# A two-layer decoder trunk: token-tile flow between the layers, and all conditioning pieces summed by VectorE

## The chip, the cores and the metric

The kernel runs on one core of a Trainium2 chip. The metric is the device time of one execution in microseconds (us). Three runs of the kernel before took 1729.4, 1731.59 and 1733.0 us.

## The reference, cut to what matters

The reference computes two layers (DEPTH = 2) over 512 tokens of width 1024, all in f32. A conditioning vector c of 1024 numbers is multiplied in each layer with a matrix `ada_w` of 1024 x 6144. The product, in twelve pieces of 512 columns, gives shift, scale and gate of both sub-layers:

```
mods = silu(c) @ ada_w[l] + ada_b[l]          # sh1, sc1, g1, sh2, sc2, g2: two pieces each
h  = rms_norm(x, norm_mix_w) * (1 + sc1) + sh1
x  = x + g1 * mixer(h)                        # attention + mLSTM, gated merge, one output projection
h2 = rms_norm(x, norm_ffn_w) * (1 + sc2) + sh2
x  = x + g2 * grouped_moe(h2)                 # 16 experts, two for each token
```

Each expert has three matrices of 1024 x 512 or 512 x 1024 (2 MB each), and the tokens are sorted by expert into blocks of 64 rows.

## The kernel before, in words

Five engines each run a program of their own and meet by semaphores. One loop over the layers (`Fori(0, DEPTH)`) holds a whole layer on each engine. Tokens are cut into NT = 4 tiles of 128, features into KD = 8 chunks of 128.

The head of a layer norms x tile by tile (`head_norm`: ScalarE squares, VectorE scales the sum, GpSimd takes the power -0.5, ScalarE writes the normed rows to `xn`). TensorE multiplies pieces 0 to 3 of `ada_w` with c (`head`, L868 to L886), turns them into columns, and VectorE forms the scale `A1` (`head_mod`, L1291). For layer 1 this head runs at the end of layer 0. Then the layer ends with a meeting: each engine waits for all five, clears its share of the semaphores, and waits again (`layer_end`, L351). At the start of the layer TensorE transposes `xn`, one feature chunk of all four tiles at a time into one of two PSUM banks (L912 to L917), and ScalarE and VectorE write `hT`.

The mixer's products all go through two PSUM banks, `pj[0]` and `pj[1]`, in an order written out in `group_order` (L39). Group g uses bank g % 2, and `take` (L890) makes TensorE wait until every earlier group of that bank has been freed:

```
if g >= 2:
    pe.wait_ge(pj_free[g % 2], g // 2)
return pj[g % 2]
```

The first merge loop (L1064 on TensorE, L1547 on VectorE, j = 0 to 7) makes the gate product `ga`, two steps of the mLSTM and the attention's up projection `ya`. VectorE reads `ya` out at L1557. With j = 2, 4 and 6 it first finishes a token tile of the mLSTM (`m_finish`, L1519). Then come `gb` 0 and 1 and four transposed tiles `hmT` (L1074 to L1079; read out at L1562). The second merge loop (L1080, L1564) makes `gb` and `yb`; `gb` 0 and 1 stand ahead of the loop, so `yb` 0 and `yb` 1 follow each other directly. VectorE reads `yb` out at L1568, and GpSimd adds it to the merged features (L538).

In the second merge loop VectorE also sums six conditioning pieces (4 to 9): `sum_mid` (L1538) is one `tensor_scalar` and seven `scalar_tensor_tensor` over 128 x 512. TensorE then sums over the partitions with a product with ones (L1093, or four column sums, L865), and VectorE stores the outcome (`mod_chunk`, L1320). Pieces 10 and 11 are multiplied by TensorE (`ada_group`, L902), one before the transposes of h2 and one beside the routing.

SyncE issues the loads of the weights from a list `ITEMS` (L272) into a ring of six buffers of 2 MB. It issues the experts' gate and up matrices, the parameters of the next layer (`params`, L368, before the loads of the last expert), and the four pieces for the next layer's head. GpSimd issues the experts' down matrices: for experts 0 and 2 after the second merge loop, for expert 1 when the first rows of the experts' stage have been transposed (L567 to L569). After the last block GpSimd gathers both expert rows of each tile (L576), and VectorE adds them to x (`combine`, L1713).

## Time and profile before

| | us |
|---|---|
| median of three runs | 1731.59 |
| the three runs | 1729.4, 1731.59, 1733.0 |
| span of the profiled execution | 1724.8 |
| TensorE busy | 1506.9 |
| VectorE busy | 563.9 |
| ScalarE busy | 323.4 |
| GpSimd busy | 121.8 |

The page gives no time of its own for the profiled execution beside its span; the span runs from the first to the last instruction, and the median of the runs is 6.8 us above it. In time a layer has these stages (layer 0): head to 53.4 us, projections and attention to 243, first merge loop to 347, second merge loop to 442, output projection to 497, routing and the scatter of the rows to 546, experts to 841, and the passage to the next layer to 893. Layer 1 repeats it 839.6 us later as far as the routing.

### The profile page before, as it was taken

What the parts mean: (1) busy time and instruction counts of PE and PEld (TensorE: products, weight loads), DVE (VectorE), ACT (ScalarE), POOL (GpSimd) and SP (SyncE); (2) the same over time, 40 slices, a digit from 0 to 9 for tenths busy, and PEclk for the clock granted to TensorE, in tenths of its full rate; (3) what the DMA queues carried; (4) which work ended last, traced back from release to release, by engine and by line L of the source; (5) the groups of instructions that cost most, each with busy time, mean ns of one, the idle gap of its engine ahead of it and who ended that gap; (6) DMA issues with size and microseconds to landing.
All of it is one profiled execution on the core that took longest, in us unless ns stands there. A gap on an engine that the chain in (4) does not pass through costs nothing.

```text
span 1724.8 us, 18335 instructions
## 1 busy us (share of the span) xinstructions
PE 1506.9 (87%) x5819; PEld 669.3 (39%) x5820; DVE 563.9 (33%) x1459; ACT 323.4 (19%) x809; POOL 121.8 (7%) x157
## 2 busy tenths in 40 slices
PE   4999999999983999987749999999999387999982
PEld 1544444544441333332335444454444132333330
DVE  1346432446333212111134554243642411221213
ACT  3133411200011212111132343111000121221210
POOL 1100000011101000000111000000110100000001
PEclk8999999999996999999769999999999789999996
DMA  9822111055747899999952111113563799997984
GB/s 307 338 97 98 49 49 49 13 206 173 291 142 268 268 375 379 376 388 360 322 180 98 49 49 50 49 49 108 206 224 145 292 314 381 378 354 247 310 303 165
DMA packets 160813, 366.59 MB, mean 213 GB/s; under 512 B 12433, under 2 KB 14705, under 8 KB 160753
## 3 DMA queue, kind: packets, MB, share of 16 engines
q1 hardware_dynamic: 127568, 256.26, 42.2%
q0 software_dynamic: 21664, 83.89, 12.8%
q10 hardware_dynamic: 11520, 25.70, 5.0%
q8 instruction: 31, 0.51, 0.1%
q14 instruction: 30, 0.24, 0.0%
HBM read 334.37 MB, written 31.46 MB: 212 GB/s over the span
## 4 chain that ended last, share of the span: by engine, by line
PE 69%; DMA 11%; SPq 5%; DVE 5%; issue 4%; ACT 2%; POOL 2%; ACTq 0%; DVEq 0%; POOLq 0%; PEldq 0%
PE bank L939 23%; PE bank L1160 14%; PE bank L929 11%; PE bank L1105 6%; PE bank L1172 6%; DMA weight_ring<-in_w_up_dram 6%; DMA regA<-in_w_up_dram 2%; SPq L428 2%; SPq L431 2%; SPq L371 2%; DMA weight_ring<-in_ada_w_dram 1%; PE bank L1152 1%; PE bank L999 1%; POOL expert_rows L558 1%; PE bank L988 1%
## 5 line engine op out<-in xcount | busy, mean ns | idle before, releaser
L939 PE MATMUL bank<-h_features,weight_ring 128*128 128x512 f32 x768 | 342.4, 599 | 3.1 <-ACT regB L674 1.9
L1160 PE MATMUL bank<-weight_ring,merged_features 128*64 128x512 f32 x960 | 227.2, 628 | 35.3 <-DMA weight_ring<-in_w_up_dram 28.2
L939 PEld LDWEIGHTS bank<-h_features,weight_ring 128*128 128x128 f32 x768 | 144.8, 192 | 182.7 <-issue 182.4
L929 PE MATMUL bank<-weight_ring,h_features 128*128 128x512 f32 (+1 forms) x512 | 196.1, 541 | 1.7 <-ACT h_features L628 1.7
L1703 DVE TENSOR_TENSOR merged_features<-bank,merged_features 64x512 f32<-64x512 f32 x44 | 30.5, 693 | 381.8 <-ACT merged_features L809 381.8
L1160 PEld LDWEIGHTS bank<-weight_ring,merged_features 128*64 128x64 f32 x960 | 73.5, 144 | 165.4 <-issue 160.8
L929 PEld LDWEIGHTS bank<-weight_ring,h_features 128*128 128x128 f32 x512 | 96.0, 190 | 97.0 <-issue 91.6
L1160 PE MATMUL bank<-h_features,merged_features 128*64 128x512 f32 x256 | 117.1, 612 | 11.0 <-DMA regA<-in_w_up_dram 10.0
L1160 PE MATMUL bank<-regA,merged_features 128*64 128x512 f32 x256 | 117.5, 614 | 0.0
L1105 PE MATMUL bank<-weight_ring,merged_features 128*128 128x512 f32 x256 | 110.4, 593 | 3.0 <-POOL merged_features L538 3.0
L1172 PE MATMUL bank<-weight_ring,merged_features 128*64 128x512 f32 x480 | 109.6, 598 | 1.6 <-DVE merged_features L1689 1.6
L809 ACT ACTIVATE merged_features<-bank 64x512 f32<-64x512 f32 x46 | 27.1, 589 | 367.9 <-PE bank L1160 367.9
L1152 PE MATMUL bank<-ident,merged_features 64*128 64x64 f32 x384 | 34.9, 233 | 44.5 <-DMA merged_features<-expert_rows 44.5
L800 ACT ACTIVATE merged_features<-bank,mod_cols,scale 128x64 f32<-128x64 f32 x192 | 61.9, 402 | 60.6 <-PE bank L1152 58.3
L1105 PEld LDWEIGHTS bank<-weight_ring,merged_features 128*128 128x128 f32 x256 | 48.5, 190 | 63.4 <-issue 60.2
L1544 DVE SCALAR_TENSOR_TENSOR regP<-weight_ring,c_padded,regP 128x512 f32<-128x512 f32 x84 | 63.2, 752 | 3.0
L1160 PEld LDWEIGHTS bank<-h_features,merged_features 128*64 128x64 f32 x256 | 34.8, 141 | 73.7 <-issue 73.7
L1685 DVE TENSOR_SCALAR merged_features<-bank,scale,mod_cols 128x64 f32<-128x64 f32 x192 | 52.8, 338 | 27.1 <-PE bank L1152 25.5
L1689 DVE TENSOR_TENSOR merged_features<-bank,g_rows 128x512 f32<-128x512 f32 x46 | 31.8, 692 | 89.8 <-PE bank L1172 78.9
L1152 PEld LDWEIGHTS bank<-ident,merged_features 64*128 64x128 f32 x384 | 28.2, 142 | 82.0 <-DMA merged_features<-expert_rows 44.7
L939 PE MATMUL bank<-regB,weight_ring 128*128 128x512 f32 x128 | 57.4, 594 | 1.6 <-DVE regB L1562 1.6
L939 PE MATMUL bank<-regA,weight_ring 128*128 128x512 f32 x128 | 57.6, 592 | 0.0
(304 smaller groups left out, 1376.1 us busy)
## 6 DMA issues: line engine op xcount, KB each, us to landing
weight_ring<-in_ada_w_dram SPq DMA_DIRECT2D x24, 2048.0 KB, 8.7
weight_ring<-in_w_gate_dram SPq DMA_DIRECT2D x22, 2048.0 KB, 21.1
weight_ring<-in_w_down_dram POOLq DMA_DIRECT2D x22, 2048.0 KB, 14.9
weight_ring<-in_w_up_dram SPq DMA_DIRECT2D x22, 2048.0 KB, 20.4
weight_ring<-in_w_in_dram SPq DMA_DIRECT2D x18, 2048.0 KB, 8.9
h_features<-in_w_gate_dram SPq DMA_DIRECT2D x10, 2048.0 KB, 17.4
regA<-in_w_up_dram SPq DMA_DIRECT2D x10, 2048.0 KB, 27.4
regB<-in_w_down_dram POOLq DMA_DIRECT2D x10, 1536.0 KB, 11.5
```

The source lines that it names most:

```text
L371: sp.dma_start(dst, src).then_inc(params_in, 16)
L428: sp.dma_start(gate_w[p], of(w_gate, l, e)).then_inc(w_gu[p], 16)
L431: sp.dma_start(up_w[p], of(w_up, l, e)).then_inc(w_gu[p], 16)
L800: last = ac.activation(xT[:, k, :], ps[2][:, MB * k:MB * k + MB], ACT.Identity, scale=A2[:, k:k + 1], bias=modc[:, 24 + k:25 + k])
L929: ins = te.matmul(bank[:, 0:w], hT[:, k, P * i:P * i + P], wv[:, k, :], start=(k == 0), stop=(k == KD - 1))
L939: ins = te.matmul(bank[:, :], wv[:, k, c0:c0 + P], rhs[:, k, :], start=(k == 0), stop=(k == kn - 1))
L1105: ins = te.matmul(bank[:, :], merged[:, k, P * i:P * i + P], slot("wo", k // 4, 4, D)[:, k % 4, 512 * h:512 * h + 512], start=(k == 0), st ...
L1152: ins = te.transpose(ps[(2, 6)[k % 2]][:, MB * k:MB * k + MB], xg[p][:, P * k:P * k + P], ident[MB * p:MB * p + MB, MB * p:MB * p + MB])
L1160: ins = te.matmul(ps[3][64 * part:64 * part + 64, :], xT[:, k, :], w[:, k, :], start=(k == 0), stop=(k == KD - 1))
L1172: ins = te.matmul(ps[5][64 * half:64 * half + 64, :], hxT[:, k, :], down_w[p][k][:, 512 * half:512 * half + 512], start=(k == 0), stop=(k ...
L1544: link(ve.scalar_tensor_tensor(mid_sum, w[:, k, :], cz[:, k, 0:1], mid_sum, ALU.mult, ALU.add))
L1685: last = ve.tensor_scalar(xT[:, k, :], ps[6][:, MB * k:MB * k + MB], A2[:, k:k + 1], modc[:, 24 + k:25 + k], ALU.mult, ALU.add)
```

## The change

Conditioning. All twelve pieces are now summed by VectorE in the merge loops: pieces 4 to 11 of this layer and pieces 0 to 3 of the next one (`STREAM`; in layer 1 the last four are computed too, and not used). Four pieces are summed in the first merge loop, half a piece behind each `ya`, the others in the second, one ahead of `hmT` and one behind each of `yb` 0 to `yb` 6. The pieces are loaded into the place of x and into `regA`; x is written to memory at the start of the layer and read back after the last piece. TensorE's sums over the partitions stand in `group_order` behind `ya` 2, 4 and 6, `gb` 0 and each `yb`. `mod_chunk`, which frees their bank, now stands behind the sum of a later piece. TensorE multiplies only the four pieces of layer 0's head.

Between layers. The meeting is gone: the semaphores are in two sets, and SyncE clears each when the engines have reported themselves through. At the start of a layer TensorE transposes one token tile after another into banks 4 to 7, tiles 0 and 1 first, tiles 2 and 3 between `q` 0 and `kv` 0. The weights `q` and `kv` of layer 1 are loaded at the end of layer 0.

Experts. Down matrices of experts 0 and 1 are loaded after the second merge loop and of expert 2 after the output projection. The parameters of the next layer are loaded at the start of the experts' stage. The two experts of a token are now ordered by their slot; the rows of the lower one are gathered when expert 14's blocks are stored. The gate weights are worked out behind the slots and tables.

```diff
+STREAM = [(0, c) for c in range(HEAD_ADA, 12)] + [(1, c) for c in range(HEAD_ADA)]
+N_HALVED = 4
+ADA_AT = {("ya", 2): 0, ("ya", 4): 1, ("ya", 6): 2, ("gb", 0): 3, ("yb", 0): 4, ("yb", 1): 5, ("yb", 2): 6, ("yb", 3): 7,
+          ("yb", 4): 8, ("yb", 5): 9, ("yb", 6): 10, ("yb", 7): 11}
+ADA_SLOT = ("x", "x", "x", "x", "A", "x", "A", "x", "A", "x", "A", "x")
...
     for j in range(8):
-        o += [("ga", j), ("ya", j)]
-    o += [("gb", 0), ("gb", 1)]
+        o += [("ga", j), ("ya", j)] + sums("ya", j)
+    o += [("gb", 0)] + sums("gb", 0) + [("gb", 1)]
...
-        o += [("yb", j)]
-        if j - 1 in MID_ADA:
-            o += [("ada", MID_ADA[j - 1])]
+        o += [("yb", j)] + sums("yb", j)
...
# SyncE
+                wait_reg(sp, head_xn, l * NT + NT)
+                sp.dma_start(xsave.rearrange("(i p) d -> p i d", p=P), xs[:, :, :]).then_inc(x_kept, 16)
...
+                through(sp, "ya", 7)
+                load_ada(4)
+                summed(sp, 3)
+                load_ada(5)
                 load_gate(0, 0)
-                through(sp, "yb", 0)
...
+                through(sp, "hmT", NT - 1)
+                load(l, "wo0")
+                for n in range(6, len(STREAM)):
+                    summed(sp, n - 2)
+                    load_ada(n)
+                    if n == 7:
+                        load(l, "wo1")
+                    if n == 9:
+                        through(sp, "gb", 3)
+                        load_gate(1, 1)
+                summed(sp, len(STREAM) - 1)
+                sp.dma_start(xs[:, :, :], xsave.rearrange("(i p) d -> p i d", p=P)).then_inc(x_back, 16)
...
# GpSimd
-                through(pool, "ada", G2_ADA + 1)
-                pool.wait_ge(xt_ready, 1)
-                load_down(1, 1)
...
-                wait_reg(pool, y_out, nb * 32 + 32)
-                for i in range(NT):
-                    for k in range(2):
+                for k in range(2):
+                    wait_reg(pool, y_out, (nb if k else blocks_through(po, E - 2)) * 32 + 32)
+                    for i in range(NT):
...
# TensorE, head of layer 0
+            param_columns(0)
+            pe.wait_ge(head_read, 1)
+            head_mods()
...
# TensorE, both loops
+                def mod_sum(n):
+                    summed(pe, n)
+                    bank = take("ada", n)
+                    if STREAM[n][1] in (4, 5, 10, 11):
+                        ins = te.matmul(bank[:, :], ones[:, :], sum_buf(n), start=True, stop=True)
+                    else:
+                        ins = column_sums(bank, sum_buf(n))
+                    ins.then_inc(pj_ready, 1)
...
+                h1_transposes(0)
+                h1_transposes(1)
                 for i in range(NT):
+                    pe.wait_ge(h1_low, i + 1)
+                    pe.wait_ge(h1_high, i + 1)
                     token_group("q", i, 512)
+                    if i == 0:
+                        h1_transposes(2)
+                        h1_transposes(3)
                     token_group("kv", i, 256)
...
# VectorE, first merge loop, behind the read-out of ya
+                    sum_ada(j // 2, slice(0, 4) if j % 2 == 0 else slice(4, KD))
+                    if ("ya", j) in ADA_AT:
+                        mod_chunk(ADA_AT["ya", j])
                 m_state(15)
                 m_finish(NT - 1)
+                mod_chunk(ADA_AT["gb", 0])
+                sum_ada(N_HALVED)
                 for i in range(NT):
...
# VectorE, second merge loop, behind the read-out of yb
-                    if j - 1 in MID_ADA:
-                        mod_chunk(MID_ADA[j - 1])
-                    if j in MID_ADA:
-                        sum_mid(MID_ADA[j])
-
+                    if N_HALVED + 1 + j < len(STREAM):
+                        sum_ada(N_HALVED + 1 + j)
+                    mod_chunk(ADA_AT["yb", j])
+
+                wait_reg(dve, x_back, l * 16 + 16)
...
# VectorE, end of the layer
-                    head_mod(l + 1)
+                    head_cols(l + 1)
+                    head_mod(modn[:, :])
                     for i in range(NT):
-                        combine(i)
+                        combine(0, i)
+                    for i in range(NT):
+                        combine(1, i)
+                        ve.sem_inc(combined, 1)
                         if i:
                             head_norm(l + 1, i - 1)
                     head_norm(l + 1, NT - 1)
```

## Rows read from the trace of the kernel before

**Rows 1.** Page, part 1: busy us, share of the span, instructions
```profile
PE 1506.9 (87%) x5819; PEld 669.3 (39%) x5820; DVE 563.9 (33%) x1459; ACT 323.4 (19%) x809; POOL 121.8 (7%) x157
```

**Rows 2.** Timeline of PE and DVE, first merge loop, layer 0: start us, us, line
```profile
283.50 7.03 PE L939 MATMUL bank<-h_features,weight_ring 128*128 128x512 f32 x16
287.11 0.69 DVE L1557 SCALAR_TENSOR_TENSOR merged_features<-merged_features,bank 128x512 f32<-128x512 f32 x1 [0.23 <-DVE regP L1516]
...
334.69 7.03 PE L939 MATMUL bank<-h_features,weight_ring 128*128 128x512 f32 x16
338.26 0.69 DVE L1557 SCALAR_TENSOR_TENSOR merged_features<-merged_features,bank 128x512 f32<-128x512 f32 x1 [0.23 <-DVE regB L1509]
```

**Rows 3.** Timeline of PE and DVE, second merge loop, layer 0
```profile
347.52 0.69 DVE L1557 SCALAR_TENSOR_TENSOR merged_features<-merged_features,bank 128x512 f32<-128x512 f32 x1 [2.67 <-PE bank L939]
...
354.10 0.69 DVE L1535 TENSOR_TENSOR weight_ring<-weight_ring,fin_small 128x512 f32<-128x512 f32 x1
...
365.35 7.13 PE L939 MATMUL bank<-regB,weight_ring 128*128 128x512 f32 x16 [0.78 <-DVE regB L1562]
...
373.48 1.52 DVE L1542 TENSOR_SCALAR regP<-weight_ring,c_padded 128x512 f32<-128x512 f32 x1 [0.26 <-DVE regU L1568]
375.04 5.48 DVE L1544 SCALAR_TENSOR_TENSOR regP<-weight_ring,c_padded,regP 128x512 f32<-128x512 f32 x7
...
382.62 1.02 PE L1093 MATMUL bank<-regP,ones 128*128 128x512 f32 x2
...
390.66 3.60 PE L939 MATMUL bank<-regB,weight_ring 128*128 128x512 f32 x8
```

**Rows 4.** Timeline of all engines, passage from layer 0 to layer 1
```profile
848.36 1.00 POOL L578 DMA_INDIRECT h_features<-expert_rows,slot_index  x1 [48.29 <-DMA expert_rows<-merged_features]
...
860.76 1.29 DVE L1716 SCALAR_TENSOR_TENSOR x_tokens<-h_features,gate_weights,x_tokens 128x1024 f32<-128x1024 f32 x1 [0.24 <-DVE scale L1299]
...
874.00 0.15 DVE L1288 TENSOR_SCALAR sum_sq<-sum_sq 128x1 f32<-128x1 f32 x1 [1.13 <-ACT merged_features L600]
...
885.04 0.06 DVE L1342 MEMSET regU<- 128x6 f32 x1 [10.89 <-issue]
...
892.98 19.40 PE L929 MATMUL bank<-weight_ring,h_features 128*128 128x512 f32 x57 [0.87 <-ACT h_features L628]
```

**Rows 5.** Timeline of POOL and PE, start of the experts, layer 1
```profile
1385.47 0.80 POOL L541 DMA_DIRECT2D weight_ring<-in_w_down_dram  x1 [9.60 <-PE bank L1152]
...
1424.60 7.09 PE L1160 MATMUL bank<-weight_ring,merged_features 128*64 128x512 f32 x32
...
1441.18 8.78 PE L1160 MATMUL bank<-weight_ring,merged_features 128*64 128x512 f32 x32 [4.88 <-DMA weight_ring<-in_w_up_dram]
```

**Rows 6.** Chain of waits, 860 to 895: start us, us, what
```profile
877.31 3.32 issue
```

**Rows 7.** Windows, experts of layers 0 and 1: busy, then PEclk, DMA share, GB/s
```profile
799.00:810.00 11.00, 9.87 (x52) 4.01 (x54) 2.17 (x6) 2.24 (x6) 0.75 (x1) 1.00 1.08 333
...
1441.00:1459.00 18.00, 13.43 (x62) 5.18 (x63) 2.49 (x6) 2.26 (x6) 0.74 (x1) 0.89 1.04 385
```

**Rows 8.** Timeline of PE, last expert of layer 0
```profile
822.89 9.10 PE L1160 MATMUL bank<-weight_ring,merged_features 128*64 128x512 f32 x32 [11.07 <-DMA weight_ring<-in_w_up_dram]
```

**Rows 9.** Timeline of DVE, routing, layer 0
```profile
521.11 0.23 DVE L1645 TENSOR_TENSOR regP<-regP 128x64 f32<-128x64 f32 x1
...
522.75 0.24 DVE L1654 COPY regP<-bank 128x80 f32<-128x80 f32 x1
```

**Rows 10.** Timeline, end of layer 1
```profile
1694.48 0.69 DVE L1689 TENSOR_TENSOR merged_features<-bank,g_rows 128x512 f32<-128x512 f32 x1 [4.40 <-DMA expert_rows<-merged_features]
1699.22 1.00 POOL L578 DMA_INDIRECT h_features<-expert_rows,slot_index  x1 [39.04 <-DMA expert_rows<-merged_features]
...
1705.89 1.28 DVE L1716 SCALAR_TENSOR_TENSOR x_tokens<-h_features,gate_weights,x_tokens 128x1024 f32<-128x1024 f32 x1 [10.71 <-DMA regA<-expert_rows,slot_index]
```

**Rows 11.** Timeline of DVE, head of layer 0
```profile
28.88 0.29 DVE L1294 COPY param_cols<-bank 128x128 f32<-128x128 f32 x1
```

More of the change, by code:

```diff
@@ L295, in mix_item @@
-            if name == "wo":
-                return lay(w_out, l)[:, 512 * part:512 * part + 512, :].rearrange("a (k p) n -> p (a k) n", p=P), D, 4
-            return cols8({"ya": w_attn_up, "yb": w_mlstm_up}[name], l, 0, D), D, 4
-        def slot(name, part, k, w):
-            return ring[:, ITEMS[ITEM[(name, part)]][2], 0:k * w].rearrange("p (k n) -> p k n", k=k)
-        def before(n):
-            return [it[2] for it in ITEMS[:n]].count(ITEMS[n][2])
+                return slot(name, 8, w), cols8(w_in, l, c0, w)
@@ new lines, in _ @@
+                sp.dma_start(xsave.rearrange("(i p) d -> p i d", p=P), xs[:, :, :]).then_inc(x_kept, 16)
+                sp.wait_ge(head_sum, HEAD_ADA)
+                for name in ("mqk0", "mqk1", "mv", "mo"):
+                    load(l, name)
+                wait_reg(sp, x_kept, l * 16 + 16)
+                load_ada(0)
+                with sp.If(l == 0):
+                    sp.wait_ge(zeroed, 3)
+                    sp.dma_start(xd.rearrange("(n p) d -> p n d", p=P),
+                                 zeros.unsqueeze(1).to_broadcast([P, ROWS // P, D])).then_inc(rows_zeroed, 16)
@@ new lines, in _ @@
+                through(sp, "q", NT - 1)
+                load(l, "ga0")
+                wait_reg(sp, moe_done, l * 4 + 4)
+                for done in moe_sems:
+                    sp.sem_clear(done)
+                sp.sem_inc(moe_cleared, 1)
+                through(sp, "mqk", 7)
+                load(l, "ga1")
+                through(sp, "mv", NT - 1)
+                load(l, "ya")
+                through(sp, "mo", NT - 1)
+                load(l, "yb")
+                summed(sp, 0)
+                load_ada(1)
@@ L427, in load_gate @@
+                through(sp, "ga", 3)
+                load(l, "gb0")
+                summed(sp, 1)
+                load_ada(2)
+                summed(sp, 2)
+                load_ada(3)
+                through(sp, "ga", 7)
+                load(l, "gb1")
                 def load_gate(p, e):
@@ L449, in _ @@
                 load_up(2, 2)
+                with sp.If(l < DEPTH - 1):
+                    sp.wait_ge(x_upd, NT)
+                    params(nxt)
+                wait_reg(sp, mix_done, l * 4 + 4)
+                for done in mix_sems:
+                    sp.sem_clear(done)
+                sp.sem_inc(mix_cleared, 1)
                 with sp.Fori(1, E // BUF) as i:
@@ L1278, in hlink @@
                 dve.wait_ge(head_step, hn[0])
-            def columns(j, bank, read, lnk):
-                lnk(ve.tensor_copy(modc[:, 4 * j:4 * j + 4], bank[:, 0:4]))
-                ve.sem_inc(read, 1)
             def head_norm(t, i):
@@ L1344, in _ @@
                 link(ve.tensor_scalar(wqk[:, 0, :], wqk[:, 0, :], HD ** -0.5, None, ALU.mult))
[L1345 to L1347 removed]
+                for i in range(NT):
+                    dve.wait_ge(h1_ready, 2 * i + 2)
+                    for k in range(4, KD):
+                        ins = ve.tensor_scalar(hT[:, k, P * i:P * i + P], h1_bank(i, 1)[:, P * (k - 4):P * (k - 4) + P], A1[:, k:k + 1], modc[:, k:k + 1],
+                                               ALU.mult, ALU.add)
+                    ins.then_inc(h1_high, 1)
                 nh = HQ + HKV
@@ L1730, in _ @@
                     for i in range(NT):
-                        combine(i)
-                layer_end(dve, l, share(4))
+                        combine(0, i)
+                    for i in range(NT):
+                        combine(1, i)
+                        ve.sem_inc(combined, 1)
+                dve.sem_inc(moe_done, 1)
 def program(nc, args):
```

457 lines of the change are left out of this document (224 added, 233 removed).

## The prediction, made before the changed kernel was timed

> **What bounds the kernel now.** I read the page first: TensorE is busy 87% of the span, VectorE 33% [rows 1]. So in the mixer the question is whether each added or moved instruction makes TensorE wait, and only in the passages between stages does another engine set the pace. I then read the timeline stage by stage. The reader is to see four things. In the first merge loop VectorE reads `ya` out late where it has just finished an mLSTM tile: `ya` ends at 283.5 and is read out by 287.8, and TensorE does not mind, since the next product goes to the other bank [rows 2]. In the second loop TensorE runs without gaps, one step from 382.62 to the next `yb` at 390.66 [rows 3]. Between the layers TensorE makes no large product from about 841 to 893; what passes is gathers, additions to x, norms, the meeting and the transposes [rows 4, 6]. In the experts' stage TensorE waits for weights where experts with one block follow each other [rows 5, 8].
>
> **The first merge loop: slower.** The change puts a sum over partitions behind `ya` 2, 4 and 6. It takes one group number, so the next `ga` is three groups behind its predecessor and falls on the bank of `ya` itself, where it was on the other bank. `take` then waits for VectorE's read-out of `ya`. These are exactly the three steps with `m_finish` ahead of the read-out. For j = 2 the read-out ends at 287.11 + 0.69 = 287.8; with 0.15 to pass the semaphore `ga` starts at 287.95 where it started at 283.5, 4.45 late. For j = 6 it is 338.26 + 0.69 + 0.15 - 334.69 = 4.4 [rows 2]. The partition sum itself (1.0, as L1093 in rows 3) lies inside this wait. Three steps by 4.5 us are 13.5 a layer, 27 in all. The half sums (four operations, 3.1 by rows 3) run behind the read-out beside `ga` (7.0) and cost nothing; the bank of the partition sum is free before the next `ya`. If the wait were hidden after all, 1.0 would be left of each, 6 in all; if each is a little longer (the middle one), 30.
>
> **hmT and the second merge loop: slower.** Follow VectorE from the last `ya`, read out at 348.2 [rows 3]. Half sum 3.1: 351.3. The last mLSTM steps took 354.8 - 348.2 = 6.6: 357.9. Then the new whole sum of a piece stands ahead of `hmT`. A sum is 0.7 to 1.5 for L1542 and 5.48 for seven L1544 [rows 3], here 6.2 since GpSimd is idle: 364.2. The transposed tiles are read out in some 3 us, two of them already in banks: `yb` 0 starts at 367.4, not 365.35, 2.1 late. (Piece 4 is issued at 347.4 and has 10.5 us to land; it may be late by some us.) `yb` 0 ends at 370.85, is read out by 371.75, and now the next sum runs at once, beside GpSimd's addition of `yb` 0. That is the case of the row at 373.48, where L1542 took 1.52; 0.26 + 1.52 + 5.5 gives 379.05. Only then come `mod_chunk` and the read-out of `yb` 1, whose bank `gb` 2 needs: 380.1 against 372.3 before, 7.8 late. A further sum (7.0) and `mod_chunk` must pass before `yb` 2: 387.6 against 379.2, 8.4 late. In the five steps that follow VectorE's own period decides: from the end of a `yb`, 0.2 + 0.7 + 0.26 + 7.0 + `mod_chunk` + 0.1 is 8.5 us with columns and 9.0 with rows, until the bank of the next `yb` is free, against 8.04 now [rows 3]. Three steps by 0.45 and two by 0.98 are 3.3. Together 11.7 a layer, 23.4 in all. Bounds: 4 if only the two added partition sums a layer count, 35 if pieces also arrive 6 us late in each layer. The way of x through memory is hidden: it is read back 6 us before `wo` begins, and the first `wo` group gives another 7.
>
> **Between the layers: faster.** The head's four pieces of `ada_w` no longer load beside the last stores, nor does VectorE wait for their columns. In layer 1, where nothing loads beside them, a first store and the read-out behind it let the gathers start 4.7 after the last row block [rows 10]; I take the same here, gathers of the lower slot from 842.0 and of the upper one from 847.1, against 848.36 for all [rows 4]. From the first gather of a pair to the first addition it was 6.7 there (1699.22 to 1705.89), that is 5.4 from the second, as issues are 1.3 apart; so tile 0 gets its second addition at 852.6, where before its first began at 860.76. From 860.76 to VectorE's last norm at 874.00 it was 13.2, with eight additions of 1.3. Four of these are now ahead (5.2), of which ScalarE's squares and scalings give back about half: 10.4, so 863.0. Now a choice. VectorE's first instruction of layer 1 stands at 885.04, and the chain has "issue" from 877.31 on, when ScalarE too was done; that is 7.7 us in which nothing is waited for [rows 4, 6]. I keep these 7.7, as the loop still jumps back: VectorE resumes at 870.7, has two small operations and four read-outs of tile 0, and `q` 0 starts at 872.6. Eight transposes each of tiles 2 and 3 now stand inside the projections (2.3), and the first products after an idle stretch cost 2.0 more (9.10 against 7.09 in rows 5 and 8). 892.98 - 872.6 - 4.3 is 16.1 gained. If the 7.7 belonged to the meeting it would be some 22; if gathers and stores keep their old times, 10.
>
> The Trainium skill ("Runtime: NRT & Kernel Launch", section "Instruction fetch mechanics") says that a taken branch out of the fetched pages forces a fetch before execution goes on. By that rule the 7.7 us stay whatever is done with the meeting, and `q` 0 can't start when the first tile is ready; without it the passage would gain some 6 us more. The row at 885.04 fits the rule but can't by itself tell it from the meeting.
>
> **Other places.** Experts of layer 1: expert 1's down matrix was issued at 1385.47, into the stretch in which the transfers are the limit; 2.1 MB at 385 GB/s are 5.5 us [rows 5, 7], and the wait of 4.88 and the one of the next expert can give them back: 5.5 (between 0 and 6). Layer 0 begins with experts of two blocks, whose products cover the loads, so there this gives nothing; but the parameters leave the stretch ahead of the last expert, whose weights come 11.07 late [rows 8]. Their bytes (0.67 MB, 1.7 us) and the dip from 385 to 333 GB/s over 11 us (1.5) make 3.2 (0 to 11). Routing: seven operations leave the path between the mask and the ranks, 521.11 to 522.75 [rows 9], and four products go: 1.3 a layer, 2.6. TensorE's pieces 10 and 11 lay in its own waits: nothing. End of layer 1: the gathers run from 1695, when the block before the last is stored, instead of 1699.22, and one addition of 1.3 instead of two follows the last of them [rows 10]: 4.2 + 1.3 = 5.5 (3 to 8). Head of layer 0: the pieces are now multiplied behind the read-out of the parameters at 28.88 [rows 11] instead of from 18.8, some 4 late, and transposing by tile gives about as much back: 0, between -3 and +3.
>
> **The sum.** Slower by 27 + 23.4 = 50.4; faster by 16.1 + 5.5 + 3.2 + 2.6 + 5.5 = 32.9. The span goes from 1724.8 to 1742.3. The median of the runs stands 6.8 above the span, so 1749.
>
> **The rivals.** (A) The banks do not bite, and the passage wins. Place: TensorE's waits for banks in both loops. If late read-outs cost only the partition sums, 27 becomes 6 and the 3.3 a layer of the second loop go: 27.6 less, 1721.5. It decides once the loops lose less than 33 in all. For it speaks that VectorE is busy only 33% [rows 1], so that much of its work could be ahead; against it the numbering of the banks, which is arithmetic. (B) The waits cool TensorE. Each new wait idles it for 3.4 to 3.9 us. In layer 1 a product group after 4.88 us without work took 8.78 instead of 7.09, at a mean granted clock of 0.89 in that stretch, so part of it at the lower level of 1.2 GHz [rows 5, 7]. Five such waits a layer by 1.7 are 17: 1766. Against it: these idle times are shorter than that one. (C) The pieces arrive late. Two buffers alternate, a load is issued when a sum ends and has 15.9 us; expert weights and `wo` share the queue. If each of six loads a layer came 4 us late it would be 48 more: 1797. Against it: before, the sums in rows 3, from two buffers too, wait for no load.
>
> **Chances.** What a measurement can tell here is about 0.2%, 3.5 us. My forecast 0.60 (its own range 1735 to 1762, 0.05 of it within 3.5 us of before), (A) 0.20 (0.03 of it within), (B) 0.15, (C) 0.05. So slower 0.75, within 0.2% 0.08, faster 0.17. The range for 8 in 10 goes from 1725 to 1766.
>
> **What would show it.** Right: TensorE idle before L939's successor three times a layer in the first loop, released by VectorE's read-out of `ya`; seven VectorE sums of 7 us back to back in the second loop; `wo` starting some 25 us later relative to `q`; VectorE silent for about 7.7 us at the start of layer 1; no wait of TensorE for the meeting. Wrong: first-loop steps still 12.9 us apart at j = 2, 4, 6; VectorE resuming within 1 us of its last norm; waits for `ada_w` loads in the loops.

## The result and the profile after

The changed kernel takes 1772.49 us (median of 4 runs, 1767.85 to 1779.8) against 1730.49 (median of 4, 1729.32 to 1733.0): ratio 1.0237, 95% interval 1.0207 to 1.0267. It is 42 us slower; the forecast was 1749, in a range of 1725 to 1766. The direction was right, the size was not.

The profiled execution took 1779.8 us, with a span of 1778.2, so it stands 7 above the median of its kernel. For the stages below that means: the spans differ by 53.4 us, the medians by 42; the 11 between are differences from run to run, not effects of the change.

Page of the kernel after, busy times and the clock that TensorE was granted, in 40 slices of the span:

```profile
PE 1513.3 (85%) x5723; PEld 673.7 (38%) x5724; DVE 642.0 (36%) x1581; ACT 324.8 (18%) x825; POOL 123.9 (7%) x157
...
PEclk9999989899996899999779998999999869899996
```

The same row of the kernel before:

```profile
PEclk8999999999996999999769999999999789999996
```

TensorE has fewer products but more busy time than before [rows 1]. The clock's row shows where to look. The first merge loop of layer 0 runs from slice 6 to slice 9, and slices 6 and 8 read 8 where they read 9 before. Slice 8 holds two of the new waits. Slice 6 ends before the first of them; what is slow there is `ga` 0 (see below). Tenths over 44 us are too coarse for the rest; windows below show it.

Where the time went, each stage from start to start, in both traces:

| stage | before | after | change | forecast |
|---|---|---|---|---|
| layer 0, start to `q` 0 | 53.4 | 45.6 | -7.8 | 0, with the next row |
| layer 0, `q` 0 to `ga` 0 | 190.1 | 193.7 | +3.6 | |
| layer 0, first merge loop (to `gb` 0) | 104.3 | 126.0 | +21.7 | +13.5 |
| layer 0, `gb` 0 to `wo` | 94.6 | 112.8 | +18.2 | +11.7 |
| layer 1, both loops | 199.0 | 236.1 | +37.1 | +25.2 |
| both layers, `wo`, routing, scatter | 208.0 | 206.1 | -1.9 | -2.6 |
| layer 0, experts | 294.8 | 295.2 | +0.4 | -3.2 |
| last product to `q` 0 of layer 1 | 51.9 | 31.0 | -20.9 | -16.1, with the next row |
| layer 1, `q` 0 to `ga` 0 | 190.0 | 195.2 | +5.2 | |
| layer 1, experts, to the last product group | 304.3 | 308.2 | +3.9 | -5.5 |
| layer 1, end | 34.4 | 28.2 | -6.2 | -5.5 |

(The stages of experts end with the last product in layer 0 and with the start of the last group in layer 1; what follows is counted from there.) The loops cost 77.0 and not 50.4; the rest gives back 23.7 and not 32.9.

Timeline of the first merge loop, layer 0, kernel after (start us, us, engine, line; in brackets the idle time before it and what ended it), answering to [rows 2]:

```profile
280.74 1.02 PE L965 MATMUL bank<-regU,ones 128*128 128x512 f32 x2
...
284.35 0.69 DVE L1619 SCALAR_TENSOR_TENSOR merged_features<-merged_features,bank 128x512 f32<-128x512 f32 x1 [0.23 <-DVE regP L1587]
...
285.19 8.80 PE L998 MATMUL bank<-h_features,weight_ring 128*128 128x512 f32 x16 [3.42 <-DVE merged_features L1619]
...
312.68 1.02 PE L965 MATMUL bank<-regU,ones 128*128 128x512 f32 x2
317.51 10.13 PE L998 MATMUL bank<-h_features,weight_ring 128*128 128x512 f32 x16 [3.81 <-DVE merged_features L1619]
...
350.50 8.80 PE L998 MATMUL bank<-h_features,weight_ring 128*128 128x512 f32 x16 [3.45 <-DVE merged_features L1619]
```

The waits stand where the forecast put them: behind the partition sum of `ya` 2, 4 and 6, ended by the read-out of `ya`, and with the sum itself 13.7 us in layer 0 and 13.6 in layer 1, against 13.5 foreseen. What it did not count is the second number of these rows: the product group behind the wait takes 8.80 and 10.13 us instead of 7.03. Windows over two of these groups and one between them (busy times, then the granted clock, DMA share, GB/s):

```profile
285.20:294.00 8.80, 8.80 (x18) 3.82 (x19) 3.19 (x5) 0.00 (x0) 0.00 (x0) 0.81 0.01 2
299.80:306.80 7.00, 7.00 (x19) 3.10 (x18) 3.61 (x5) 0.00 (x0) 0.00 (x0) 1.00 0.42 130
317.50:327.60 10.10, 10.09 (x18) 4.29 (x19) 3.20 (x5) 0.00 (x0) 0.00 (x0) 0.70 0.01 2
```

Mean clock 0.81 and 0.70 with the transfers quiet: part of each group ran at 1.2 GHz and the rest at 2.4, right behind 3.4 to 3.8 us without a product. Three groups cost 1.77 + 3.10 + 1.77 = 6.6 us in layer 0. In layer 1 the first of the three takes 8.80 too, and the other two:

```profile
1180.92 8.51 PE L998 MATMUL bank<-h_features,weight_ring 128*128 128x512 f32 x16 [3.78 <-DVE merged_features L1619]
...
1212.27 9.89 PE L998 MATMUL bank<-h_features,weight_ring 128*128 128x512 f32 x16 [3.42 <-DVE merged_features L1619]
```

That is 6.1 us, and here the longer wait has the faster group: the cost of one wait scatters between 1.5 and 3.1 us and does not follow its length.

`ga` 0 is slow without any wait. It stands ahead of the first added sum, behind products with four rows; first the kernel before, then the kernel after:

```profile
243.48 8.73 PE L939 MATMUL bank<-h_features,weight_ring 128*128 128x512 f32 x16
```

```profile
232.51 5.40 PE L1095 MATMUL bank<-merged_features,ident 4*128 4x512 f32 x8 [0.25 <-ACT weight_ring L776]
...
239.34 9.97 PE L998 MATMUL bank<-h_features,weight_ring 128*128 128x512 f32 x16
```

From 231.0 to 239.3 TensorE of the changed kernel is busy for 8.05 of 8.30 us at a mean clock of 0.73. In the twelve kernels of this study `ga` 0 takes between 8.6 and 10.2 us, in either layer, and the products of four rows ahead of it 3.9 to 5.6. In this pair of profiles the place costs 2.1 us in the stage `q` 0 to `ga` 0 and 1.2 in the first loop more than before. The instructions there are the same in both kernels, and e6 (below) is back at 3.94 and 8.79. I count these 3.3 us as scatter and not as an effect of the change; what sets them no run shows.

Second merge loop, kernel after, answering to [rows 3]:

```profile
384.64 5.40 PE L998 MATMUL bank<-regB,weight_ring 128*128 128x512 f32 x8 [0.78 <-DVE regB L1629]
...
391.03 1.52 DVE L1404 TENSOR_SCALAR regP<-x_tokens,c_padded 128x512 f32<-128x512 f32 x1 [0.26 <-DVE regU L1635]
...
398.58 1.74 PE L921 MATMUL bank<-ones,regP 128*128 128x1 f32 x8 [3.94 <-DVEq L1393]
400.18 9.76 PE L998 MATMUL bank<-h_features,weight_ring 128*128 128x512 f32 x16
...
422.71 3.67 PE L998 MATMUL bank<-regB,weight_ring 128*128 128x512 f32 x8 [1.23 <-DVEq L1393]
```

Again the foreseen waits (the partition sum behind `yb` 1, and each later `yb` behind `mod_chunk`, L1393) and slow products: `yb` 0 5.40 instead of 3.60, behind three short waits of the transposes and of itself (0.34, 0.95 and 0.78 us), the partition sum behind `yb` 1 1.74 instead of 0.95, `gb` 2 9.76 instead of 7.03. That is 5.3 us; 18.2 less 5.3 is 12.9 against 11.7 foreseen. In layer 1 `yb` 0 takes 3.70 behind nearly the same three waits (0.34, 0.92 and 0.78), the sum 1.84 and `gb` 2 9.23, so that only 3.1 us are lost to the clock there.

The passage, kernel after, answering to [rows 4]:

```profile
878.42 1.00 POOL L635 DMA_INDIRECT h_features<-expert_rows,slot_index  x1 [38.85 <-DMA expert_rows<-merged_features]
...
884.06 1.28 DVE L1788 SCALAR_TENSOR_TENSOR x_tokens<-h_features,gate_weights,x_tokens 128x1024 f32<-128x1024 f32 x1 [5.19 <-DMA h_features<-expert_rows,slot_index]
...
900.89 0.15 DVE L1338 TENSOR_SCALAR sum_sq<-sum_sq 128x1 f32<-128x1 f32 x1 [2.25 <-ACT merged_features L657]
...
905.50 0.06 DVE L1410 MEMSET regU<- 128x6 f32 x1 [4.46 <-issue]
...
907.51 1.22 PE L987 MATMUL bank<-weight_ring,h_features 128*128 128x512 f32 x1 [5.73 <-ACT h_features L680]
```

The gathers begin 1.9 us behind the last product (876.5), the last norm stands at 900.9, and VectorE resumes 4.46 us later, waiting for nothing that the profile shows.

Experts of layer 1, kernel after, answering to [rows 5, 7]:

```profile
1441.75 9.46 PE L1216 MATMUL bank<-weight_ring,merged_features 128*64 128x512 f32 x32 [1.38 <-ACT merged_features L857]
...
1518.56 1.08 PE L1216 MATMUL bank<-h_features,merged_features 128*64 128x512 f32 x1 [14.58 <-DMA regA<-in_w_up_dram]
```

Expert 5's up matrix is waited for 14.58 us, where before expert 4 waited 4.88 [rows 5] and expert 5 4.39:

```profile
1458.96 1.08 PE L1160 MATMUL bank<-h_features,merged_features 128*64 128x512 f32 x1 [4.39 <-DMA regA<-in_w_up_dram]
```

The end of layer 1, kernel after, answering to [rows 10]:

```profile
1753.68 1.00 POOL L635 DMA_INDIRECT h_features<-expert_rows,slot_index  x1 [33.85 <-DMA expert_rows<-merged_features]
...
1767.32 1.28 DVE L1788 SCALAR_TENSOR_TENSOR x_tokens<-regA,gate_weights,x_tokens 128x1024 f32<-128x1024 f32 x1 [1.98 <-DMA regA<-expert_rows,slot_index]
```

The lower slot's gathers and additions run ahead of the last stores, as foreseen (6.2 against 5.5).

### The profile page after: what moved, and what is told of

It is laid out like the page before. It is cut to its first block, busy times and chain, and to the rows that moved or that the text cites. A ratio compares the mean times of both kernels' runs of the same rounds, so it can differ in the third digit from the quotient of the medians.

```text
span 1778.2 us, 18326 instructions
## 1 busy us (share of the span) xinstructions
PE 1513.3 (85%) x5723; PEld 673.7 (38%) x5724; DVE 642.0 (36%) x1581; ACT 324.8 (18%) x825; POOL 123.9 (7%) x157
## 4 chain that ended last, share of the span: by engine, by line
PE 63%; DMA 13%; DVE 11%; issue 6%; ACT 3%; POOL 2%; SPq 1%; DVEq 0%; POOLq 0%; ACTq 0%
PE bank L998 18%; PE bank L1216 15%; PE bank L987 11%; DMA weight_ring<-in_w_up_dram 8%; PE bank L1228 6%; PE bank L1164 5%; DVE regP L1406 3%; DMA regA<-in_w_up_dram 2%; PE bank L1208 1%; DVE regP L1404 1%; DMA expert_rows<-merged_features 1%; PE bank L1065 1%; SPq L469 1%; DMA regA<-expert_rows,slot_index 1%; PE bank L1054 1%
## 5 line engine op out<-in xcount | busy, mean ns | idle before, releaser
L998 PE MATMUL bank<-h_features,weight_ring 128*128 128x512 f32 x768 | 363.1, 628 | 24.5 <-DVE merged_features L1619 21.3
L1216 PE MATMUL bank<-weight_ring,merged_features 128*64 128x512 f32 x960 | 229.7, 634 | 27.4 <-DMA weight_ring<-in_w_up_dram 20.3
L998 PEld LDWEIGHTS bank<-h_features,weight_ring 128*128 128x128 f32 x768 | 151.2, 201 | 215.3 <-issue 214.9
L1216 PE MATMUL bank<-h_features,merged_features 128*64 128x512 f32 x256 | 116.1, 607 | 21.9 <-DMA regA<-in_w_up_dram 20.9
L1216 PEld LDWEIGHTS bank<-weight_ring,merged_features 128*64 128x64 f32 x960 | 73.5, 145 | 160.0 <-issue 155.3
L1228 PE MATMUL bank<-weight_ring,merged_features 128*64 128x512 f32 x528 | 120.6, 598 | 1.6 <-DVE merged_features L1762 1.6
L1208 PEld LDWEIGHTS bank<-ident,merged_features 64*128 64x128 f32 x384 | 28.2, 142 | 80.2 <-DMA merged_features<-expert_rows 42.9
L1228 PEld LDWEIGHTS bank<-weight_ring,merged_features 128*64 128x64 f32 x528 | 35.4, 136 | 60.1 <-issue 58.0
## 6 DMA issues: line engine op xcount, KB each, us to landing
weight_ring<-in_w_gate_dram SPq DMA_DIRECT2D x22, 2048.0 KB, 14.8
```

Source lines behind the costliest of these rows:

```text
L998: ins = te.matmul(bank[:, :], wv[:, k, c0:c0 + P], rhs[:, k, :], start=(k == 0), stop=(k == kn - 1))
L1208: ins = te.transpose(ps[(2, 6)[k % 2]][:, MB * k:MB * k + MB], xg[p][:, P * k:P * k + P], ident[MB * p:MB * p + MB, MB * p:MB * p + MB])
L1216: ins = te.matmul(ps[3][64 * part:64 * part + 64, :], xT[:, k, :], w[:, k, :], start=(k == 0), stop=(k == KD - 1))
L1228: ins = te.matmul(ps[5][64 * half:64 * half + 64, :], hxT[:, k, :], down_w[p][k][:, 512 * half:512 * half + 512], start=(k == 0), stop=(k ...
```

## The experiments

The theory: the loss is the bank of `ya`, held by a late read-out, and each such wait also costs clock. The rivals: it is the summing itself that makes VectorE late; the slow products have another cause than the wait. Ratios are to the kernel before, run on the same chip; the changed kernel's is 1.0237.

**The partition sums moved (e1).** VectorE sums as much, at the same places; only the groups of TensorE and their read-outs move.

```diff
-ADA_AT = {("ya", 2): 0, ("ya", 4): 1, ("ya", 6): 2,
+ADA_AT = {("ya", 3): 0, ("ya", 5): 1, ("ya", 7): 2,
```

> The changed kernel with the three partition sums of the first merge loop behind ya 3, 5 and 7 instead of ya 2, 4 and 6; nothing else. ga still falls on the bank of the ya before it, but no mLSTM tile is finished ahead of these read-outs. Theory (late read-out of ya holds the bank, and each such wait also drops TensorE's clock): the three waits of 3.4 to 3.8 us a layer fall to 0.3 or less and the product behind them goes from 8.80, 10.13 and 8.80 us back to 7.03; 10.7 + 6.6 a layer, 34 in all, so some 1738. Rival (the bank alone is enough, wherever the sum stands): the waits stay at about 3 us, no more than 5 us faster. Rival (VectorE's half sums make it late, not the mLSTM tile): the waits move with the sums, time unchanged.

1735.56 us, ratio 1.0005 (0.9983 to 1.0028): 37 us faster than the changed kernel by the medians, 40 by the ratios. Timeline, first merge loop and start of the second, layer 0:

```profile
292.67 1.02 PE L965 MATMUL bank<-regU,ones 128*128 128x512 f32 x2
293.70 7.10 PE L998 MATMUL bank<-h_features,weight_ring 128*128 128x512 f32 x16
...
366.14 3.70 PE L998 MATMUL bank<-regB,weight_ring 128*128 128x512 f32 x8 [0.79 <-DVE regB L1629]
...
378.38 1.02 PE L921 MATMUL bank<-ones,regP 128*128 128x1 f32 x8 [3.94 <-DVEq L1393]
379.30 8.79 PE L998 MATMUL bank<-h_features,weight_ring 128*128 128x512 f32 x16
```

No wait for a bank and no slow group but `ga` 0 (8.68) is left in the first loop, which takes 107.9 us; `ga` still falls on the bank of the `ya` before it, but that read-out is prompt. The rival "VectorE's half sums" falls, and so does "any sum behind `ya`". The transposed tiles `hmT` wait as little as in the kernel before (0.34 and 0.36 us), since VectorE reaches them in step with TensorE: the sum ahead of `hmT` costs nothing here. The spans of the two profiles differ by 44 us, more than the 34 expected; some 4 of these are `ga` 0 of both layers and `yb` 0 of layer 0 (3.70), places that scatter.

**The wait filled with products (e2).**

```diff
                     bank = take("ada", n)
+                    if n < 3:
+                        for _ in range(3):
+                            te.matmul(bank[:, :], ones[:, :], sum_buf(n), start=True, stop=True)
```

> The changed kernel with three more products of ones with the summed rows (128x512, overwritten by the sum that counts) ahead of each of the three partition sums of the first loop, so that TensorE works through most of the wait for the bank. They take 3 x 0.86 = 2.6 us of a wait of 3.4 to 3.8. Theory (the clock drops because TensorE idles in the wait): the next ga goes from 8.80 to 10.13 us back to about 7.03, 6.6 a layer, 13 faster in all, so some 1759, although more work is done. Rival (the slow products are contention or the bank, not the clock): ga stays at 8.8 or more, no change.

1763.83, ratio 1.0156 (1.0115 to 1.0197): 9 us faster by the medians, 14 by the ratios, though TensorE does more. Timeline, first merge loop, layer 0:

```profile
280.93 2.74 PE L966 MATMUL bank<-regU,ones 128*128 128x512 f32 x6
283.50 1.02 PE L968 MATMUL bank<-regU,ones 128*128 128x512 f32 x2
285.38 7.11 PE L1001 MATMUL bank<-h_features,weight_ring 128*128 128x512 f32 x16 [0.85 <-DVE merged_features L1622]
...
316.00 7.11 PE L1001 MATMUL bank<-h_features,weight_ring 128*128 128x512 f32 x16 [1.23 <-DVE merged_features L1622]
```

`ga` starts as late as before for the same bank and the same read-out, and takes 7.11. So the slow group is the idle time's, not the bank's. From the sum's start to the group's end it is 11.6, 11.9 and 11.5 us against 13.3, 15.0 and 13.2: 6.4 in layer 0. The three groups of layer 1 take 7.1 too. Together with e1, a wait of 3.4 to 3.8 us costs 5.2 to 6.9.

**Small groups alone, in the kernel before (e3 and e4).** Four column products of ones behind `ya` 2, 4 and 6, one group or two; no pieces, loads or sums.

```diff
-        o += [("ga", j), ("ya", j)]
+        o += [("ga", j), ("ya", j)] + [("ms", 1 * j + k) for k in range(1) if j in (2, 4, 6)]
...
# TensorE, behind ya
+                            bank = take("ms", 1 * j + k)
+                            for q in range(4):
+                                ins = te.matmul(bank[:, q:q + 1], ones[:, :], ones[:, 0:1], start=True, stop=True)
```

> The kernel before with one small group (four column products of ones, 1.0 us) put behind ya 2, 4 and 6, freed by VectorE at once; no pieces, loads or sums are added, and its outcome is not used. Theory: the next ga now falls on the bank of ya: a wait of about 3.4 us and a slower product each time, 6 x (4.5 + 2.2) = 40 slower than before, so some 1770. By the waits alone, as in the forecast: 27 slower, 1757. If only the added products count: 6 slower.

1774.51, ratio 1.0215 (1.0174 to 1.0257): slower than the kernel before by 42 us by the medians and 37 by the ratio, with 40 expected.

```profile
284.15 0.95 PE L1075 MATMUL bank<-ones 128*128 128x1 f32 x8
288.59 8.71 PE L939 MATMUL bank<-h_features,weight_ring 128*128 128x512 f32 x16 [3.49 <-DVE merged_features L1563]
...
320.81 9.66 PE L939 MATMUL bank<-h_features,weight_ring 128*128 128x512 f32 x16 [3.89 <-DVE merged_features L1563]
```

Six groups of 0.95 us, whose outcome is not used, cost about as much as the whole change did (42 and 41 us by the same two measures): waits and slow products as in the changed kernel, with VectorE as free as it was.

> The same with two such groups behind ya 2, 4 and 6, so that ga is back on the other bank. Theory: the second group waits for the bank of ya instead, so the wait can only be less if groups are counted; the second group of the pair falls on ya's own bank and waits for its read-out as ga did, 3.4 us, then ga follows at once on a bank that is free: about as slow as with one group (40 slower) or 1.0 us more each, 46. Rival (only which bank ga takes matters, small groups pass): two cost 12 us, less than one.

1788.69, ratio 1.0303 (1.0259 to 1.0348): 57 slower by the medians, 52 by the ratio, more than the 46 expected.

```profile
289.91 1.86 PE L1075 MATMUL bank<-ones 128*128 128x1 f32 x8 [3.40 <-DVE merged_features L1563]
291.64 9.56 PE L939 MATMUL bank<-h_features,weight_ring 128*128 128x512 f32 x16
```

An even number of groups does not help: the second one waits for `ya`'s bank in place of `ga`, runs at the low clock itself (1.86 instead of 0.95), and `ga` behind it takes 9.56 instead of 8.71. From the start of the first small group to the end of `ga` the six places take 15.5 to 16.0 us each, against 13.1 to 14.8 in e3: 12 us more in all, where 6 were expected.

**Second loop: `mod_chunk` ahead of the next sum (e5, on top of e1).**

```diff
+                    mod_chunk(ADA_AT["yb", j])
                     if N_HALVED + 1 + j < len(STREAM):
                         sum_ada(N_HALVED + 1 + j)
-                    mod_chunk(ADA_AT["yb", j])
```

> The kernel with the moved partition sums, and in the second merge loop VectorE reads the partition sum out (mod_chunk) ahead of the next piece's sum instead of behind it. Theory (each yb waits for the bank that the partition sum holds, because mod_chunk stands behind 7 us of summing): the waits of 1.2, 1.2, 0.5, 0.5 and 0.5 us ahead of yb 3 to 7 go, 3.9 a layer, 8 faster than the kernel with the moved sums, some 1728; the wait of 3.9 ahead of the partition sum behind yb 1 stays, as it is for the sum itself. Rival (VectorE has too little time for a sum a step, so the wait moves to the partition sum): no change.

1728.55, ratio 0.9976 (0.9955 to 0.9998): 7 faster than e1 by the medians, 5 by the ratios, whose intervals overlap; 8 expected. In the traces the stretch from `yb` 0 to `yb` 7 takes 78.8 us instead of 84.2, in both layers. The waits ahead of `yb` 3 to 7 are gone, the one behind `yb` 1 stays:

```profile
377.25 1.05 PE L921 MATMUL bank<-ones,regP 128*128 128x1 f32 x8 [3.54 <-DVEq L1408]
378.26 8.80 PE L998 MATMUL bank<-h_features,weight_ring 128*128 128x512 f32 x16
...
398.36 3.60 PE L998 MATMUL bank<-regB,weight_ring 128*128 128x512 f32 x8
```

**The sums spread by operations (e6, on top of e5).** No operation between `yb` 0 and `yb` 1, then nine or ten in each step.

```diff
+SHARE = (0, 9, 9, 9, 9, 10, 10, 0)
...
+                    at = sum(SHARE[:j])
+                    while at < sum(SHARE[:j + 1]):
+                        to = min((at // KD + 1) * KD, sum(SHARE[:j + 1]))
+                        sum_ada(N_HALVED + 1 + at // KD, slice(at % KD, to - at // KD * KD))
+                        at = to
```

> The same, and the seven pieces of the second loop are cut by operations: none between yb 0 and yb 1, where no gb gives VectorE time, then 9, 9, 9, 9, 10 and 10 operations behind yb 1 to yb 6 (the last two partition sums both stand behind yb 7). Theory: the wait of 3.9 us behind yb 1 and the slower product behind it (8.8 instead of 7.1) go as well, 5.6 a layer, 11 faster than with the order alone, some 1716; each step then has some 10 us of VectorE in 11.7. Rival (VectorE becomes the bound at ten operations a step, or pieces arrive late from two buffers): waits of 1 to 2 us at each step, 1725 or more.

1714.13, ratio 0.9908 (0.9891 to 0.9926): faster than both kernels. `gb` 2 follows `yb` 1 at once and at full clock, and the longest wait in the loop is 0.22 us:

```profile
371.34 7.03 PE L999 MATMUL bank<-h_features,weight_ring 128*128 128x512 f32 x16
...
382.80 7.11 PE L999 MATMUL bank<-h_features,weight_ring 128*128 128x512 f32 x16 [0.22 <-DVEq L1638]
```

The two loops now take 205.3 us in layer 0 and 206.1 in layer 1, 6.3 and 7.1 more than in the kernel before, which is about the six added partition sums. So all of the loss in the loops, but for the sums on TensorE, was order.

**Where the experts' gain went (e7, e9, on top of e6).**

```diff
# e7, GpSimd
-                load_down(1, 1)
...
+                pool.wait_ge(xt_ready, 1)
+                load_down(1, 1)
# e9, GpSimd
                 def next_down(p, e):
+                    wait_reg(pool, gu_ready, blocks_through(po, e - BUF + 2))
                     wait_reg(pool, y_ready, blocks_through(po, e - BUF))
```

> The kernel with the spread sums, and expert 1's down matrix loaded as in the kernel before, when the first rows of the experts' stage have been transposed. By the forecast's premise (these 2.1 MB then fall into the stretch where transfers are the limit) 5.5 us slower in layer 1. By what the traces now suggest (at the start of the stage the transfers run at 220 to 254 GB/s against 385 later, so the load falls into a gap): no change, within 2 us, and the wait for expert 5's up matrix stays near 14 us.

1714.87, ratio 0.9905 (0.9881 to 0.9929): no change. The preload of expert 1's down matrix saves nothing, and the wait for expert 5's up matrix in layer 1 is 14.22 us, against 12.26 in e6. The 20 us from the first expert group of layer 1 on, first in e6, where the matrix is there already, then in e7, where it is loaded in them, show why:

```profile
1374.50:1394.50 20.00, 16.83 (x61) 5.69 (x63) 1.79 (x5) 3.51 (x7) 0.00 (x0) 0.69 0.83 245
```

```profile
1377.87:1397.87 20.00, 16.80 (x60) 5.70 (x62) 1.79 (x5) 3.52 (x7) 0.70 (x2) 0.69 1.01 331
```

With the load the transfers are at their limit (DMA share 1.01, 331 GB/s), without it they have room (0.83, 245), and nothing moves up into the room: the next gate matrix is issued 10.1 us behind the start of the first group in both. The kernel before and the changed kernel show the same pair, 332 and 253 GB/s.

> The kernel with the spread sums; GpSimd issues each down matrix one expert later (when the gate and up products of the expert ahead of it are done), so that it competes less with the gate and up matrices of SyncE's queue, which are needed first. Theory (the wait of 12 to 15 us for expert 5's up matrix in layer 1 comes from down matrices that are moved beside it although they are not needed yet): the wait falls by 5 us or more and the experts' stage of layer 1 gets 3 to 6 us shorter, some 1709. Rival (the bytes in all are the limit there, their order does not matter): waits only change their place, no change. Rival (the down matrices then come late): new waits in both layers, 5 to 20 us slower.

1717.61, ratio 0.9912 (0.9886 to 0.9939), no different from e6. In layer 1 the wait for expert 5's up matrix halves, from 12.26 us in e6, and in layer 0 a new one opens:

```profile
702.06 1.09 PE L1219 MATMUL bank<-h_features,merged_features 128*64 128x512 f32 x1 [11.84 <-DMA regA<-in_w_up_dram]
...
1447.99 1.09 PE L1219 MATMUL bank<-h_features,merged_features 128*64 128x512 f32 x1 [6.25 <-DMA regA<-in_w_up_dram]
```

The up matrix arrives 69.6 us after the first group instead of 77.5, yet the whole stage is as long as in e6 (308.7 and 308.9 us to the last group): the order of the two queues decides where the wait falls and not how long the stage is. What does decide its length no run isolated. Why the kernels of this family need 308 to 310 us there and the kernel before 304.3 was not settled. The Trainium skill ("DMA: Bandwidth & Descriptors", section "Queues, rings and completion order") says that each DMA engine takes packets in turn from the queues that have work; the 7.9 us by which this up matrix arrives earlier when the down matrices step back agree with it.

**Early gathers undone (e8, on top of e6).**

```diff
-                    wait_reg(pool, y_out, (nb if k else blocks_through(po, E - 2)) * 32 + 32)
+                    wait_reg(pool, y_out, nb * 32 + 32)
```

> The kernel with the spread sums, but the gathers of the lower slot wait for the last stores too, as all gathers did in the kernel before. If the early gathers carry part of the gain of the passage, the eight gathers at 1.3 us apart end 5 us later and the time grows by 4 to 5 us in the passage and by as much at the end of layer 1, 8 to 10 in all. If the additions or norms set the pace: under 3.

1720.86, ratio 0.9944 (0.9924 to 0.9964): 6.7 slower than e6, a little under the 8 to 10 expected for the two places. In the traces each place is 3.1 us longer: 33.7 instead of 30.6 from the last product to `q` 0 of layer 1, and 31.5 instead of 28.4 at the end of layer 1. `q` 0 of layer 1 still waits for the same chain of additions and norms, which starts later.

**TensorE kept busy in two other waits (e10, on top of e6).**

```diff
+                for k in range(12):
+                    te.matmul(ps[7][:, :], ones[:, :], gate_w[0][:, k % KD, :], start=True, stop=True)
                 pe.wait_ge(xg_in[0], 16)
...
                 h1_transposes(1)
+                arrived(pe, "q")
+                for k in range(3):
+                    te.matmul(pj[GI[("q", 0)] % 2][:, :], ones[:, :], slot("q", 8, 512)[:, k, :], start=True, stop=True)
```

> The kernel with the spread sums; TensorE fills two of its waits with products whose outcome is not used: twelve of 128x512 while it waits for the first rows of the experts' stage (20 us), three ahead of q 0 of each layer. Theory (a product group behind an idle stretch is slow because the granted clock fell in it): the first two gate and up groups (9.6 to 9.8 us now) and q 0 (8.8 to 10.2) come near 7.1; in layer 0 this is 5 us in the experts' stage, where products are the limit, nothing in layer 1, where transfers are, and 2 for each q 0: 5 to 9 us faster, some 1707. Rival (fillers too far from the end of the wait do not help, or delay it): within 2 us.

1712.07, ratio 0.9867 (0.9838 to 0.9896): 2 us faster than e6 by the medians, 7 by the ratios, whose intervals overlap. `q` 0 of layer 1, first in e6, then in e10 with the fillers ahead of it:

```profile
868.55 10.21 PE L988 MATMUL bank<-weight_ring,h_features 128*128 128x512 f32 x16 [5.67 <-ACT h_features L681]
```

```profile
865.26 4.05 PE L1006 MATMUL bank<-weight_ring,ones 128*128 128x512 f32 x6
...
871.16 7.13 PE L988 MATMUL bank<-weight_ring,h_features 128*128 128x512 f32 x16 [1.84 <-ACT h_features L681]
```

10.21 us became 7.13, although TensorE idled 1.84 between the fillers and the group. The first expert group of layer 0 went from 9.55 in e6 to 7.09 too; the second one, behind a further wait of 1.99, takes 8.78, where in e6 it takes 7.09 behind 2.05. By its median this is the fastest kernel of the study; that it is faster than e6 is not clear of noise.

## Why the forecast was right in direction and wrong in size

**The first merge loop.** Mechanism, places and length of the waits were right (13.7 and 13.6 against 13.5 a layer). The term was mis-sized all the same: the forecast priced a wait at its length, 4.5 each, and the group behind it lost another 1.5 to 3.1. Measured 21.7 in layer 0, of which 1.2 are the scatter of `ga` 0. The forecast had this loss as rival (B), at 1.7 for each of five waits a layer, and gave it 0.15 with the argument that 3.4 to 3.9 us are shorter than the 4.88 in [rows 5]. That step failed: one row at 4.88 us shows that such an idle time is enough, not that a shorter one is too little. (B) should have been part of the likeliest case, and its size was 11.9 in layer 0 (6.6 in the first loop, 5.3 in the second) and 9.2 in layer 1 (6.1 and 3.1), 21 in all and not 17.

**hmT and the second loop.** 12.9 without the clock, in both layers, against 11.7: `yb` 0 1.7 late, 3.9 us behind `yb` 1, then half a microsecond to 1.2 at each `yb`, by `mod_chunk` behind a sum. The 1.7 are for the most part the added partition sum behind `gb` 0 (0.95) and a longer wait at `hmT`; VectorE's sum ahead of `hmT` turned out not to be a cost of its own (e1).

**The passage.** Right, in part by luck. `q` 0 came 20.9 us nearer to the last product, 20.4 foreseen, and the stage behind it grew by 5.2 instead of 4.3. Of these 5.2 only 3.3 are the transposes inside the projections and the slower first group (8.69 instead of 7.1); 2.0 are the products of four rows ahead of `ga` 0, which the forecast did not count. And the gathers and additions took longer than assumed (last norm 24.4 us after the last product, 22.0 assumed), and the idle time at the loop's start was 4.46, not 7.7. The two misses, 2.4 and 3.2 us, cancel but for 0.8. If the jump back cost the same before, the 7.7 [rows 4, 6] were about 4.5 of it and some 3 of the meeting; no run took the meeting away alone. The rule of the Trainium skill that was named there ("Runtime: NRT & Kernel Launch", section "Instruction fetch mechanics") agrees with the trace so far: VectorE idles between 4.44 and 4.55 us there in the changed kernel and in all eight experiments that start from it, and `q` 0 does not start before VectorE is back. That it is the fetch of instructions, no run showed.

**The experts' stage.** Two terms failed, 8.7 us in sum, which came out as 4.3 lost. The gain of 5.5 in layer 1 rested on the premise that expert 1's down matrix was loaded where transfers are the limit, so that its bytes would be given back to later loads. The 385 GB/s of the sum were read some 55 us behind that load [rows 7]. Where it was made the transfers were at their limit too, but because of this load; without it no later load is issued earlier, and the time is the same (e7). For the 3.2 in layer 0 no experiment was made.

**Routing, end, head.** 1.9 against 2.6, 6.2 against 5.5, and 4.2 gained ahead of the first loop where 0 was forecast, outside its 3.

**The sum.** 17.5 was forecast and 53.3 is the difference of the spans. Of the missing 36, 26.6 are the loops (21 of these are the slow groups behind the new waits, 2.5 the scatter of `ga` 0, and 3 the waits themselves); 13 are the experts' stage; 4 came back ahead of the first loop. The range ended at rival (B) added to the forecast with every gain kept, 1766; with the experts' gain gone as well the median lies 6.5 above it. Rival (A) was wrong about the banks, but right that VectorE has time enough: with the same sums in another order (e6) the kernel takes 1714.

## What to carry to other kernels

Where groups alternate between two banks, an added group, however small, shifts which read-out the next large product waits for; number the groups before and after, and put the new one where the read-out ahead of it is prompt. Price a wait of TensorE not by its length alone: add what the rows show of a group behind a wait of that size (here 1.5 to 3.1 us behind 3.4 to 3.9), and if the wait can't go, fill it with products of full width as in e2 (the column products of e4 did not help). Before a preload is credited with its bytes, ask which later load would be issued earlier once they are gone: where every later load waits for a buffer to come free, none is.

## What the runs showed of the hardware

Idle times of 3.4 us already cost clock, and what one costs scatters. In the changed kernel and in e3, in both layers, a group of 7.03 us took 8.7 to 9.9 behind 3.40 to 3.49 us, and 8.5 to 10.1 behind 3.78 to 3.89. Behind 0.82 to 1.23 us, with products of 128x512 ahead (e2), it took 7.1, and behind 1.84 us (e10) 7.13. Behind some 2 us it came out either way: the second expert group of layer 0, 7.09 us at full clock, took 7.09 in the kernel before (1.97 us) and in e6 (2.05), 8.78 in e10 (1.99) and 9.69 in e7 (2.05).

The clock also fell while TensorE was busy. `ga` 0 took 8.6 to 10.2 us in all twelve kernels with no idle time right ahead of it, behind products with four rows; in the changed kernel the mean clock over the 8.3 us ahead of it was 0.73. In e4 the column products behind the wait took 1.5 to 1.9 us instead of 0.95, and the large groups behind them 9.28 to 10.02, against 8.71 to 9.98 straight behind the wait in e3.

The first operation of a sum on VectorE took 0.48 us with GpSimd idle and 1.52 where it started together with GpSimd's addition (391.03 above); where it began 0.3 or 0.9 us behind the addition's start, in the kernel before, it took 1.21 and 0.69. The seven operations behind it took 5.48 each time, so a sum is 6.0 or 7.0 us by its neighbour.
